# Two transformer blocks on one core: earlier weight splits, single waits in three stages, and a norm whose tiles come straight from the sum

## The reference

```
x = first_block(x, ...)                 # two layers, modulated by c
    per layer: x += 0.5 * g * swiglu(norm(x))      stages f0, f2 (hidden width 2816)
               x += g * mixer(norm(x))             sb: stick-breaking attention, 16 heads; lru: gated linear recurrence
               x += 0.5 * g * swiglu(norm(x))      stages f1, f3
    x = rmsnorm(x, final_norm_g)
x = second_block(x, ...)                # stages h0 and h1
    per layer: h = rmsnorm_2(x, norm_g_2); proj = h @ w_in; three kinds of attention (24 heads), each gated;
               merged = sum over the three of sigmoid(m_g) * (y @ w_branch);  x = x + merged @ w_out
    return rmsnorm_2(x, final_norm_g_2)
```

## Time and profile before

| | us |
|---|---|
| median of three runs | 3413.18 |
| the profiled execution | 3413.44 |
| its span, first to last instruction | 3411.6 |
| PE busy in it | 3226.3 |

### The profile page before, as it was taken

How to read it: one execution, slowest core, us unless ns; L and a number is a source line. 1 busy time by engine, 2 the same in 40 slices (tenths; PEclk the granted TensorE clock), 3 DMA queues, 4 the chain that set the end, 5 groups by cost and what they waited for, 6 DMA issues and landing times.

```text
span 3411.6 us, 38726 instructions
## 1 busy us (share of the span) xinstructions
PE 3226.3 (95%) x16353; PEld 2666.2 (78%) x16353; DVE 1769.3 (52%) x2488; ACT 1167.0 (34%) x1526; POOL 166.2 (5%) x228
## 2 busy tenths in 40 slices
PE   6999989999999999999999998889989998899998
PEld 5887877788888888887888887666768886567687
DVE  6555542355555643367633335776643458755434
ACT  4222355542222312247432232233442232335322
POOL 0000011110000000001100000000000010000000
PEclk8999999999999999999999998989989999899899
DMA  5555421125554443231333323221213232222131
GB/s 218 193 177 180 141 75 50 50 73 175 184 186 148 149 148 99 90 112 50 99 99 99 99 74 93 75 62 50 81 50 99 74 104 79 66 62 75 50 99 68
DMA packets 287270, 354.23 MB, mean 104 GB/s; under 512 B 9546, under 2 KB 263290, under 8 KB 287098
## 3 DMA queue, kind: packets, MB, share of 16 engines
q1 hardware_dynamic: 287098, 351.75, 31.8%
HBM read 336.52 MB, written 2.10 MB: 99 GB/s over the span
## 4 chain that ended last, share of the span: by engine, by line
PE 81%; DVE 10%; ACT 6%; issue 1%; POOL 1%; DMA 1%; SPq 0%; DVEq 0%; ACTq 0%; POOLq 0%
PE psum L591 57%; PE psum L730 6%; PE psum L688 3%; PE psum L1152 3%; PE psum L1021 2%; PE psum L612 2%; PE psum L1059 2%; DVE w_low L1725 1%; PE psum L824 1%; PE psum L1037 1%; DVE psum L1874 1%; DVE area L2188 1%; PE psum L557 1%; DVE h_low L1884 1%; PE psum L684 1%
## 5 line engine op out<-in xcount | busy, mean ns | idle before, releaser
L591 PE MATMUL psum<-h_high,w_high 128*128 128x512 f32 (+1 forms) x2496 | 990.0, 397 | 50.9 <-DVE w_low L1725 21.4
L591 PE MATMUL psum<-h_low,w_high 128*128 128x512 f32 (+1 forms) x2496 | 981.7, 393 | 0.0
L591 PE MATMUL psum<-h_high,w_low 128*128 128x512 f32 (+1 forms) x2496 | 980.8, 393 | 0.0
L1725 DVE TENSOR_TENSOR w_low<-raw,w_high 128x2048 fp32r<-128x2048 f32 (+2 forms) x246 | 546.3, 2228 | 307.8 <-ACT w_high L1210 307.6
L1210 ACT CAST w_high<-raw 128x2048 fp32r<-128x2048 f32 (+3 forms) x254 | 464.3, 1840 | 530.9 <-DMA raw<-in_ffn_w_gu 237.1
L591 PEld LDWEIGHTS psum<-h_high,w_high 128*128 128x128 f32 (+1 forms) x2496 | 474.5, 190 | 162.1 <-issue 35.2
L591 PEld LDWEIGHTS psum<-h_high,w_low 128*128 128x128 f32 (+1 forms) x2496 | 474.0, 190 | 101.7
L591 PEld LDWEIGHTS psum<-h_low,w_high 128*128 128x128 f32 (+1 forms) x2496 | 474.7, 190 | 99.0 <-issue 1.0
L591 PE MATMUL psum<-y_high,w_high 128*128 128x512 f32 x592 | 234.0, 395 | 11.2 <-DVE w_low L1725 8.6
L1995 DVE TENSOR_TENSOR area<-area,psum 128x512 f32<-128x512 f32 x88 | 60.2, 684 | 342.4 <-PE psum L591 334.0
L591 PE MATMUL psum<-y_low,w_high 128*128 128x512 f32 x592 | 232.4, 393 | 0.0
(11 more groups left out here) (294 smaller groups left out, 4403.7 us busy)
## 6 DMA issues: line engine op xcount, KB each, us to landing
raw<-in_ffn_w_gu SPq DMA_DIRECT2D x88, 1024.0 KB, 5.9
raw<-in_mod_w SPq DMA_DIRECT2D x64, 1024.0 KB, 5.0
raw<-in_w_in SPq DMA_DIRECT2D x64, 1024.0 KB, 5.2
raw<-in_ffn_w_down SPq DMA_DIRECT2D x32, 1024.0 KB, 7.5
raw<-in_ffn_w_down SPq DMA_DIRECT2D x16, 768.0 KB, 4.9
raw<-in_sb_w_qkv SPq DMA_DIRECT2D x12, 1024.0 KB, 5.2
area<-area SPq DMA_DIRECT2D x92, 128.0 KB, 2.3
raw<-in_lru_w_in SPq DMA_DIRECT2D x10, 1024.0 KB, 5.3
```

The source lines that it names most:

```text
L591: mm = e.matmul(psum[0:width, base + m, :], wv[a][:, at_k, c0:c0 + width], X[b][:, k, :], start=(at_k == 0 and (a, b) == (0, 0)), stop=(at ...
L1725: e.tensor_tensor(w_low[raw_at[m]][:, :n], raw[raw_at[m]][:, :n], w_high[x % NW][:, :n].bitcast(F32), ALU.subtract).then_inc(*q.up(s_low, ...
```

## The change

In the vector table a new column set both_gains is made once, the product of the first block's final gain and h0's gain.

In sb the query and key products of pairs 1, 3 and 5 are made output tile by output tile (`product_tiles`), each tile with a semaphore of its own, and ACT copies them tile by tile (`kept_tile`), the query's between the casts of the two heads. ACT and DVE take the stream two panels ahead of the named one instead of one.

In lru's last round ACT takes the panels (back, 0, 2) and (back, 0, 3) before the exponentials, and DVE takes panels earlier in its list, one of the large ones ahead of `power` and not after it.

Into h0 DVE scales the sum itself by both_gains and by the product of the two inverse roots; the first block's result is written into xT by eight instructions per half behind `spread` of the second half and behind `apply` of it. The gathering of the second half stands after item 13 of the first panel's products and not after item 8, and the PSUM tiles are given free by the last scaling and the last remainder.

In h0 and h1 six of the eight tiles of merged are split ahead of the last round's multiplications on DVE, and ACT waits for the last m_g product instead of the end of the round on all engines.

decay moves from f0 to f2, between the takes of gate 12 and up 12.

```diff
         n_vec += n
-col["c_act"], col["decay"] = n_vec, n_vec + KD
-assert col["decay"] + NB <= 336
+col["c_act"], col["decay"], col["both_gains"] = n_vec, n_vec + KD, n_vec + KD + NB
+assert col["both_gains"] + KD <= 336
...
+def two_ahead_of(i):
+    return min(i + 2, len(panels) - 1)
...
 def gain_of(name, j):
-    return {"end1": lambda: v("final_norm_g", j), "h0": lambda: v("norm_g_2", j), "h1": lambda: v("norm_g_2", KD + j)}.get(name, lambda: gain_in[:, j:j + 1])()
+    return {"end1": lambda: v("final_norm_g", j), "h0": lambda: v("both_gains", j), "h1": lambda: v("norm_g_2", KD + j)}.get(name, lambda: gain_in[:, j:j + 1])()
...
+    def product_tiles(key, X, x_ready, ks):
+        i, w, total = w_views(*key)
+        take(i)
+        base = base_of[key] = only[0]
+        wv = [x[:, :total].rearrange("p (k n) -> p k n", n=PANEL) for x in w]
+        wait_panel(i)
+        for m in range(2):
+            wait_free(base + m)
+            for at_k, k in enumerate(ks):
+                for h in range(2):
+                    for step in x_ready(k, h):
+                        q.wait_ge(*at(*step))
+                for a, b in COMBOS:
+                    mm = e.matmul(psum[:, base + m, :], wv[a][:, at_k, m * P:(m + 1) * P], X[b][:, k, :],
+                                  start=(at_k == 0 and (a, b) == COMBOS[0]), stop=(at_k == len(ks) - 1 and (a, b) == COMBOS[-1]))
+            mm.then_inc(*q.up(s_product, "product_tile", *key, m))
+        q.mark("w_done", i)
+        return base
...
                     if h == 0 and stage != "f0":
-                        if (p, at_) == (0, 8):
+                        if (p, at_) == (0, 13 if stage == "h0" else 8):
...
         for bank in range(2):
-            free[pair_of(to_norm, 0) + bank] = [("normed", to_norm, 1)]
+            free[pair_of(to_norm, 0) + bank] = [("scaled", to_norm, 1, KD - 1), ("h_low", to_norm, KD - 1, 1)]
...
             key = (stage, part, u)
-            b = product_tokens(key, H, hr, PANEL) if part == 2 else product(key, H, hr, range(KD), PANEL)
-            free_pair(b, ("qkv", part, u))
+            if part == 2:
+                free_pair(product_tokens(key, H, hr, PANEL), ("qkv", part, u))
+                return
+            b = product_tiles(key, H, hr, range(KD))
+            for m in range(2):
+                free[b + m] = [("qkv_tile", part, u, m)]
...
                     free_pair(base, ("merge_gate", stage, "m_g", o))
+            if jj == KD // 2 - 1:
+                q.mark("h_read", stage)
...
                     take(gate)
+                    if (stage, c0) == ("f2", 12):
+                        decay()
...
                     n += 1
-            if (stage, row) == ("f0", KD):
-                decay()
...
         e.preload_act_table_set("natural_log_exp_and_others")
+        def kept_tile(part, u, m):
+            key = (stage, part, u)
+            q.wait_ge(*at("product_tile", *key, m))
+            if u > 1:
+                q.wait_ge(*at("sb_scores", 2 * u - 3))
+            e.mul((sb_q, sb_k)[part][u % 2][:, m, :], psum[:, base_of.get(key, 0) + m, :], SCALE if part == 0 else 1.0).then_inc(
+                *q.up(s_taken, "qkv_tile", part, u, m))
+            if m:
+                q.mark("qkv", part, u)
         for p in range(PAIRS):
+            u = (p + 1) // 2
+            both = len(SB_BESIDE.get(p, ())) == 2
...
                 e.copy(sb_high[x], sb_sp[x]).then_inc(*q.up(s_act, "sb_high", p, x))
+                if both and x == 0:
+                    kept_tile(0, u, 0)
+                    kept_tile(0, u, 1)
             for part, u in SB_BESIDE.get(p, ()):
-                take((stage, part, u))
-                kept(part, u)
+                split_to(two_ahead_of(number[stage, part, u]))
+                if part == 2:
+                    kept(part, u)
+            if both:
+                kept_tile(1, u, 0)
+                kept_tile(1, u, 1)
...
-        def recur(n0):
+        def recur(n0, between=()):
...
                     *q.up(s_act, "lru_is", n))
+            for key in between:
+                take(key)
...
                 pad(n0 + 2)
-            recur(n0)
+            recur(n0, () if more else [(stage, "back", 0, 2), (stage, "back", 0, 3)])
...
                 take((stage, "gate", n0 + 2))
-            else:
-                for c in range(2, NC):
-                    take((stage, "back", 0, c))
...
         q.mark("past", (stage, "merged"), "ACT")
-        fence(q, (stage, "merged"))
+        q.wait_ge(*at("h_read", stage))
...
             q.wait_ge(*at("past", "consts", "POOL"))
+            if which:
+                e.tensor_tensor(root, root, stats[0][:, 4 + HT * h:4 + HT * (h + 1)], ALU.mult).then_inc(*q.up(s_norm))
+                q.wait_ge(*q.newest)
...
-        def ended(name, j):
-            q.wait_ge(*at("x", name, j, h))
-            e.scalar_tensor_tensor(xT[:, j, hs], xT[:, j, hs], gain_of(name, j), spread_inv[0], ALU.mult, ALU.mult).then_inc(
-                *q.up(s_norm, "final", name, j, h))
         def scaled(j):
-            if name == "h0":
-                ended("end1", j)
-                q.mark("x", "h0", j, h)
-            q.wait_ge(*at("x", name, j, h))
+            q.wait_ge(*at("x", source_of(name), j, h))
...
                 scaled(j + 1)
-                if j + 1 == KD - 1:
+                if j + 1 == KD - 1 and name != "h0":
...
             rest(j)
+    def ended(h):
+        for j in range(KD):
+            x = xT[:, j, HALF[h]]
+            e.scalar_tensor_tensor(x, x, gain_of("end1", j), psum[:, norm_bank("h0", h), 0:S // 2], ALU.mult, ALU.mult).then_inc(
+                *q.up(s_norm, "normed", "h0", h))
+            q.mark("x", "h0", j, h)
...
             spread(stage, 1)
+            if stage == "h0":
+                ended(0)
...
             split_to(i + 3)
+        if stage == "h0":
+            ended(1)
...
                     take(gate)
+                    if (stage, c0) == ("f2", 12):
+                        decay()
...
                 out_gain(stage)
-            if (stage, row) == ("f0", KD):
-                decay()
...
             for part, u in SB_BESIDE.get(p, ()):
-                take((stage, part, u))
+                split_to(two_ahead_of(number[stage, part, u]))
...
                 take((stage, "x", n0 + 2))
+            else:
+                take((stage, "back", 0, 0))
...
             else:
-                project_back(stage, 0, x_of(stage), panels_of=range(NC - 1))
+                project_back(stage, 0, x_of(stage), panels_of=range(2))
+                take((stage, "back", 0, 3))
+                project_back(stage, 0, x_of(stage), panels_of=range(2, 3))
...
+        def merged_low(j):
+            q.wait_ge(*at("h_read", stage))
+            q.wait_ge(*at("merged_high", stage, j))
+            e.tensor_tensor(H[1][:, j, :], L.merged[:, j, :], H[0][:, j, :].bitcast(F32), ALU.subtract).then_inc(*q.up(s_vec, "merged_low", stage, j))
...
             dst = L.merged[:, 2 * jj:2 * jj + 2, :]
+            if jj == KD // 2 - 1:
+                for j in range(2 * jj):
+                    merged_low(j)
...
         fence(q, (stage, "merged"))
-        for j in range(KD):
-            q.wait_ge(*at("merged_high", stage, j))
-            e.tensor_tensor(H[1][:, j, :], L.merged[:, j, :], H[0][:, j, :].bitcast(F32), ALU.subtract).then_inc(*q.up(s_vec, "merged_low", stage, j))
+        for j in range(KD - 2, KD):
+            merged_low(j)
...
     gains("f0")
+    e.tensor_tensor(v("both_gains", 0, KD), v("final_norm_g", 0, KD), v("norm_g_2", 0, KD), ALU.mult).then_inc(*q.up(s_vec, "both_gains"))
```

## The result

The changed kernel takes 3380.75 us (median of four, 3371.75 to 3388.01) against 3409.45 in the same measurement (four, 3405.5 to 3429.3): ratio 0.9899, 95% interval 0.9861 to 0.9938. It is faster by about 1%, inside the forecast range and 8.5 us above the forecast of 3372.3. Its profiled execution is 3387.83 us, span 3386.1; that of before had a span of 3411.6. The difference of the spans is 25.5, where the sum had 41.1.

The account below looks back on a forecast made before the run. PE bounds the kernel, busy 3226.3 of 3411.6 us, so only its waits and slow clock count. Terms 24.8 + 5.8 + 3.4 + 0.5 + 6.8 - 0.2 = 41.1 us off 3413.44 give 3372.3; range 3361 to 3390.

Parts of the forecast that it names:

- sb: Key products at p = 1, 3, 5: three 5.76 us waits for w_low and slow clock behind go; 24.8 us gain.
- The first rival: Waits go but the slow clock stays behind other short pauses; 30.2 us remain, 3383 us; chance 0.12.
- the second: In sb a new wait of about 5.5 us, at a bank or the weighing, replaces the 5.76; 3397 us; chance 0.08.
- The rule beside it: In sb, counting half of each throttled stretch as lost would add up to 3 x 2.9 us (sum 49.8, not 41.1).
- decay: Moving its DVE chain from f0 to f2 removes PE's 3.92 us wait and the slow product behind: 5.8 us gain.
- Into h0: Passage into h0 without overwriting in DVE's chain: second half 2.8 us, first 0.6; 3.4 us gain, range 1 to 5.7.
- The 0.6 for the first half: Into h0, six overwrites leave the front of the squares the gathering waits for; 0.6 us gain, bounds -1 and 2.9.
- The last eight overwrites: Into h0, standing ahead of DVE's first rotation and the query product, they were to cost 0.
- lru: Lru's end: 3.71 us wait for w_low goes, y_low comes 1.4 earlier; 0.5 us gain, bounds -2 and 3.
- The slow product that I took off: At lru's end, a slow stretch expected behind PE's new wait for y_low, costing about 1 us.
- Merging: 4.24 us wait before w_out shrinks or goes: h1 gains 5.6, h0 1.2 because a bank holds it; together 6.8 us.
- Setup: The product of the gains, one more small DVE operation ahead of f0's first tiles, costs 0.2 us.

Follow-up runs that it names:

- experiments 3 and 4: Changed kernel, sb's edit halved: first whole query and key products and copies, two panels ahead, 3393.18 us; then by tiles, one panel ahead, 3396.02 us.
- experiment 5: Changed kernel with the gathering of the second half into h0 after item 8 again instead of 13: 3387.75 us.
- experiment 6: Changed kernel with lru's end as in the kernel before, all else changed: 3392.29 us.
- experiment 7: Changed kernel with three tiles of merged split ahead of the last round's multiplications instead of six, five behind: 3372.83 us, ratio 0.9864.
- Experiments 1 and 2: Reruns without an edit: first the changed kernel, six runs, 3378.22 us, ratio 0.9885; then the kernel before, one more profile, 3428.97 us.
- the pair: Same idle products filling PE's waits at index scores and heads, added to the kernel before (3405.03 us) and to the changed kernel (3368.5 us).

## Why the prediction was right, and where it missed

The time fell inside the range and the direction holds. By the steps of the prediction:

- **sb, 24.8 forecast, 23.5 measured.** The term as it was made up came to the tenth: the key products of before take 13.74, 13.34 and 13.13, those of after 10.9 without a wait, so 3 x 5.76 + 2.8 + 2.4 + 2.2 = 24.7. The missing 1.3 are lost at sb's first scores: 16 matmuls behind a wait of 2.03 that both kernels have take 2.43 in the profile of before and 3.71 in that of after. That is no chance of one run: the stretch has 7.2 in all nine profiles with the whole edit of sb and 5.6 in the five without it or with one half. The granted clock falls to 0.50 behind that wait in the nine and not in the five; why the edit brings this about is not shown. No wait for a bank or a copy arose, and experiments 3 and 4 show that the distances in the argument were what the edit lives on. The first rival (the slow clock stays) and the second (a new wait) didn't come.
- **The rule beside it.** TensorE: Matmul & The Clock Gate, part 1, in the Trainium skill, counts a throttled stretch as a loss of half its length. The prediction made up to 33.5 of it for sb, with half of each wait added; that is more than the rule gives here. The three slow stretches are 6.8 long each in the profile of before and begin some 1.3 to 2.6 us ahead of the product, so by the rule, as an estimate, they cost 3.4 each and sb 27.5. The trace disagrees by less: they cost 2.8, 2.4 and 2.2. The prediction's reading, that only what PE multiplies in a slow stretch counts, holds.
- **decay, 5.8 forecast, 6.1 measured** up to sb: 5.8 at the product of f0 and 0.3 in the passage into sb, for which the prediction has no term. f2, where it went, has the same length to 0.1.
- **Into h0, 3.4 forecast, 4.9 measured** up to the heads, of which 3.6 in the passage itself. The second half went as forecast: from DVE's first tile at 2055.70 to 2064.4, 8.7 us. The 0.6 for the first half was a balance that the prediction didn't see: moving the gathering behind tile 6 makes DVE wait for PE and costs over 1 us (experiment 5); without it the first half gives about 2.5 (5.3 less the second half's 2.8), near its bound of 2.9. The last eight overwrites, put at 0, cost 1.8: ACT's copy for the rotation waits for them, and PE for the rotation. The prediction had looked at DVE's own first rotation and at the query product, not at ACT's copy. That the stretch came out above the forecast all the same is the clock in the index scores, and luck.
- **lru, 0.5 forecast, 1.8 measured**, confirmed by experiment 6. The chain to y_low sets the end, as forecast, and comes 1.8 earlier, not 1.4. A wait of 3.46 stands where 3.71 and 0.49 stood, but 0.66 of the first is left, and the slow product between them has gone. The slow product that I took off behind the new wait, 1 us, doesn't show in the profile of after; it does in those of experiments 3 and 4 (12 matmuls take 5.46 in place of 2.97 in experiment 3, 0.9 by the end of the next wait), so the term is right for some runs and not for others.
- **Merging, 6.8 forecast, 7.2 measured.** h1 5.8 for 5.6. h0 waits 2.75 for the bank (forecast 3.0), and experiment 7 gets 3.0 us of the rest back.
- **Setup, 0.2 forecast, 0.3 measured**, within the 1.2 us by which the profiles differ there among themselves.

The total lies in the range, but not because each step held. What failed is a step of the sum that no term names: that the stretches without an edit keep the time of the one profile. The places with an edit gave what was forecast and somewhat more, and the heads of h0 and h1 took 17.6 of it back in the profiled execution. Experiments 1 and 2 show that it isn't the change's doing as such: the same kernel, before or after, runs these heads in a short or in a long form, some 7.7 us apart in each layer. The profile of before had the short form in both layers, that of after the long form in both. The prediction named the spread of the runs of before, up to 24 us, but used it for the lower end alone and didn't ask where in the kernel it lies. The weak end of the terms left room for the 8.5 us above the forecast; it was made for edits that give less than forecast, and these didn't, so that the room sufficed is luck.

Over all runs of the unedited kernels here the medians are 3414.6 (46 of before) and 3378.2 (10 of after), 36.4 apart; the shortest are 3404.9 and 3371.8, 33.1 apart; with the waits filled 36.5. The edited places give 40.1 in the first two profiles, if only the new wait of 1.8 is counted behind h0's passage and not its balance with the clock, and 41.4 in the pair, where 1.5 are clock and idle products fill most of that wait. So 4 to 5 us by the medians, and 7 by the shortest runs, stay lost in stretches that weren't edited; in the pair 4.2 of them are placed, in h1's heads, where the clock is what differs. Why one form comes and not the other was not settled: the waits ahead are equal to 0.05 us in both, and no run here brings either form about at will; the filled waits only keep the long one away. The Trainium skill (TensorE: Matmul & The Clock Gate, part 1) says that the ramp to the full clock varies from run to run of one kernel, and with it the count of slow matmuls. The rows above agree: the same 8 scores of h0 take 3.02 and 3.62 us behind the same wait in two profiles of the kernel before.

## What to carry to other kernels

Before a profile is used as the base of a sum, look for groups of matmuls that stand behind waits like those here (1.9 to 3.2 us) and at their granted clock, and ask what they would take at the other clock: here such groups in two layers are worth 15 us from run to run, over a third of what the edits gained. Then compare the stretches that weren't edited, before any gain is put down to an edit. Where two waits end close together, as the panel and the bank in sb, only removing both pays (4.8 and 1.6 alone, 23.5 together). Idle products paid in the waits ahead of the index scores and the first head (13.8 us here, where 3.84 us of them took up most of a wait of 4.28), gained nothing by themselves in the last part of the heads, where 5.52 stood in a wait of 3.19, and cost their full length where there was no wait. Work moved out of a chain, like the overwrites here, must be followed to everyone who waits for the engine that now does it later.

## What was unexpected of the hardware

- Behind a wait of 3.19 us the same 8 scores took 3.02, 3.62 or 4.63 us in different executions, and 2.42 with the wait filled.
- A whole layer's heads switched between two lengths 7.7 us apart, each layer by itself, in one and the same kernel.
- Behind a wait of 2.03 us in sb the clock fell to 0.50 in nine profiles and stayed at 1.00 in five, and the only difference is whether the whole edit of sb is in the kernel (the stretch takes 7.2 or 5.6 us).
- A product behind a wait of 3.15 us took 12.77 or 14.03 in two kernels that have the same instructions there, and 10.9 undisturbed.
- A higher mean clock came with a longer time (0.982 and 3368.56 against 0.980 and 3359.04), since the products that raised it took their own time.
